# The expert loop of a decoder step: 17 turns for 18, with the used turns in the middle

## The reference

```python
def moe(h, w_router, b_router, wg, wu, wd):
    ...
    _, idx = lax.top_k(jnp.where(in_grp, sel, -jnp.inf), TOP_K)
    p_sel = jnp.take_along_axis(probs, idx, axis=-1)
    w = p_sel / jnp.sum(p_sel, axis=-1, keepdims=True)
    gates = jnp.sum(jax.nn.one_hot(idx, N_EXPERTS, dtype=jnp.float32) * w[..., None], axis=1)
    a = jnp.einsum('nd,edf->nef', t, wg)
    b = jnp.einsum('nd,edf->nef', t, wu)
    act = jax.nn.silu(a) * b * gates[:, :, None].astype(t.dtype)
    return jnp.einsum('nef,efd->nd', act, wd).reshape(shape)
```

## Time and profile before

| | |
|---|---|
| runs | 1200.85, 1202.0, 1206.45 us; median 1202.0 |
| profiled execution | span 1199.4 us from the first to the last instruction; the page gives no other time of its own for it |
| TensorE busy | 1143.6 us (95%) |
| VectorE, ScalarE, POOL busy | 618.3, 339.4, 256.3 us |
| first matmul of the loop, start of the last tile on TensorE | 804.16, 1170.61 us |
| one step of TensorE in the loop | 22.5 us |
| weight transfers in the loop, issue to landing | up 8.5, gate 9.7, down 14.0 us (medians) |
| waits of ScalarE's L1404 for TensorE | 186.4 us in 18 |
| executions of POOL's scatter L1013 | 17 |

### The profile page before, as it was taken

The page is one execution under the profiler, slowest core; times in us unless marked ns, Lnnn a source line. Parts: engine busy times, 40 slices in busy tenths (PEclk is TensorE's granted clock), DMA queues, the critical chain, the costliest instruction groups (busy, mean ns, idle before and its releaser), DMA issues.

```text
span 1199.4 us, 19161 instructions
## 1 busy us (share of the span) xinstructions
PE 1143.6 (95%) x6692; PEld 540.0 (45%) x6692; DVE 618.3 (52%) x1255; ACT 339.4 (28%) x719; POOL 256.3 (21%) x303
## 2 busy tenths in 40 slices
PE   6999999999997999998999999999999999999995
PEld 3444444444444666665544454533333333333332
DVE  0010676867779899999985574831121122122111
ACT  2132221222107888888412232100000000000000
POOL 2011102210218930000010010122223223222222
PEclk8999999999998999999999999999999999999998
DMA  9942243223328455744623356699968697968983
GB/s 358 350 151 75 98 127 116 78 97 97 98 78 277 157 195 167 239 155 162 231 87 106 105 172 224 247 343 336 352 239 315 228 359 285 352 233 295 350 292 136
DMA packets 114100, 250.76 MB, mean 209 GB/s; under 512 B 14446, under 2 KB 28910, under 8 KB 113000
## 3 DMA queue, kind: packets, MB, share of 16 engines
q1 hardware_dynamic: 93345, 206.85, 49.6%
q0 software_dynamic: 16704, 38.30, 9.1%
q10 hardware_dynamic: 3984, 4.72, 1.2%
HBM read 370.93 MB, written 38.17 MB: 341 GB/s over the span
## 4 chain that ended last, share of the span: by engine, by line
PE 68%; DVE 11%; DMA 9%; issue 6%; ACT 3%; SPq 2%; POOL 0%; POOLq 0%; DVEq 0%; ACTq 0%
PE bank L1612 21%; PE bank L2022 16%; PE bank L2036 7%; PE bank L1803 7%; DMA low<-out_dram,o_col 3%; PE bank L1592 3%; DVE big L2304 2%; DMA out_dram<-mid,o_col 2%; DVE big L2314 2%; PE bank L1467 2%; DVE cvT L2355 2%; DMA big<-in_w_up_dram 1%; PE bank L1674 1%; PE bank L2012 1%; DMA h_d<-low 1%
## 5 line engine op out<-in xcount | busy, mean ns | idle before, releaser
L2022 PE MATMUL bank<-big,mid 128*64 128x512 f32 x1104 | 251.1, 595 | 2.1 <-DMA big<-in_w_gate_dram 1.9
L1612 PE MATMUL bank<-big 128*128 128x512 f32 x560 | 249.2, 598 | 0.1
L1612 PEld LDWEIGHTS bank<-big 128*128 128x128 f32 x560 | 103.6, 190 | 131.3 <-issue 131.3
L2199 DVE SCALAR_TENSOR_TENSOR cvT<-low,cw,cvT 128x256 f32<-128x256 f32 x360 | 156.9, 512 | 0.0
L2022 PEld LDWEIGHTS bank<-big,mid 128*64 128x64 f32 x1104 | 78.1, 137 | 147.3 <-issue 147.3
L2036 PE MATMUL bank<-big,mid 128*64 128x512 f32 x544 | 119.6, 592 | 0.0
L2304 DVE TENSOR_TENSOR_SCAN big<-big 128x513 f32<-128x513 f32 (+4 forms) x96 | 91.5, 992 | 4.8 <-ACT big L1208 4.7
L2915 DVE TENSOR_TENSOR mid<-bank,low 128x512 f32<-128x512 f32 x34 | 21.9, 686 | 112.8 <-PE bank L2036 57.2
L899 POOL TENSOR_TENSOR st<-st,mhalf 128x16 f32<-128x16 f32 (+1 forms) x9 | 25.2, 2802 | 252.6 <-DVE st L2230 243.8
L2896 DVE TENSOR_TENSOR xt<-xt,bank 128x512 f32<-128x512 f32 x18 | 12.4, 688 | 126.6 <-ACT xt L1409 125.3
L2036 PEld LDWEIGHTS bank<-big,mid 128*64 128x64 f32 x544 | 39.1, 137 | 77.7 <-issue 77.7
(11 more groups left out here) (463 smaller groups left out, 1407.4 us busy)
## 6 DMA issues: line engine op xcount, KB each, us to landing
big<-in_w_gate_dram SPq DMA_DIRECT2D x38, 2048.0 KB, 9.7
big<-in_w_up_dram SPq DMA_DIRECT2D x37, 2048.0 KB, 8.5
big<-in_w_down_dram SPq DMA_DIRECT2D x37, 2048.0 KB, 14.0
low<-in_w_ada_dram SPq DMA_DIRECT2D x32, 512.0 KB, 4.1
low<-in_cache_v_dram SPq DMA_DIRECT2D x64, 256.0 KB
big<-in_w_in_dram SPq DMA_DIRECT2D x8, 1280.0 KB, 17.3
xt<-in_x_prompt_dram SPq DMA_DIRECT2D x16, 512.0 KB, 4.7
mid<-in_w_ada_dram SPq DMA_DIRECT2D x8, 1024.0 KB, 13.9
```

Of the source, the lines that this page charges most:

```text
L1612: mm = pe.matmul(bank[:, 4 if cc == 2 else cc, :], hT[:, s, k, :], w_in_sb[:, k, cc * 512:(cc + 1) * 512], start=(k == 0), stop=(k == KD - 1))
L2022: mm = pe.matmul(bank[half, 2 * s + w, :], xgT[:, s, k, half], held[x][:, k, :], start=(k == 0), stop=(k == KD - 1))
L2199: c.put(V.scalar_tensor_tensor(out, src, cw[:, ch, tap:tap + 1], out, ALU.mult, ALU.add))
```

## The change

The loop has 17 turns, and the branch in it asks whether the turn lies in a window of `pairs_used` turns, which starts at `first = (17 + 1 - pairs_used) >> 1`. `inside` tests both ends at once: each of two sums has bit 5 or higher set where its end holds. Inside the loop the number of pairs done so far comes from a register of its own, `done`, counted up at the end of a used turn, and no longer from `i`.

```diff
+        PAIRS_MAX = MP // 2 - 1
+
+        def window(pairs_used):
+
+            first = (PAIRS_MAX + 1 - pairs_used) >> 1
+            return 32 - first, first + pairs_used + 31
+
+        def inside(i, at):
+            return ((at[0] + i) & (at[1] - i)) >= 32
+
+        def counter(eng):
+
+            done = nc.alloc_registers("pairs_done", engines=[eng.engine])
+            nc.regs_mov(done, 0)
+            return done
+
+        def reached(done):
+            return nc.snap(done, min_val=0, max_val=PAIRS_MAX - 1)
+
...
-            pairs_used = pe.value_load(n_pairs[0:1, 0:1], min_val=1, max_val=MP // 2 - 1)
+            pairs_used = pe.value_load(n_pairs[0:1, 0:1], min_val=1, max_val=PAIRS_MAX)
+            at = window(pairs_used)
+            done = counter(pe)
...
             step(0, 0, 1, (wg_sb[:, 0, :, :], wg_next))
-            with pe.Fori(0, MP // 2) as i, pe.If(i < pairs_used):
-                step(2 * i + 1, 1, i + 1)
-                step(2 * i + 2, 0, i + 2)
+            with pe.Fori(0, PAIRS_MAX) as i, pe.If(inside(i, at)):
+                j = reached(done)
+                step(2 * j + 1, 1, j + 1)
+                step(2 * j + 2, 0, j + 2)
+                nc.regs_alu(done, done, 1, op=ALU.add)
```

More of the change, by code:

```diff
@@ L810, in _ @@
             sp.wait_ge(S["tiles_ready"], 3)
-            pairs_used = sp.value_load(n_pairs[0:1, 0:1], min_val=1, max_val=MP // 2 - 1)
+            pairs_used = sp.value_load(n_pairs[0:1, 0:1], min_val=1, max_val=PAIRS_MAX)
+            at = window(pairs_used)
+            done = counter(sp)
             def refill(t, now, nxt, then, gates=None):
@@ L825, in _ @@
             sp.wait_ge(S["tiles_ready"], 4)
-            with sp.Fori(0, MP // 2) as i, sp.If(i < pairs_used):
-                e = pass_experts(pass_exp, 2 * i + 1, 4)
+            with sp.Fori(0, PAIRS_MAX) as i, sp.If(inside(i, at)):
+                j = reached(done)
+                e = pass_experts(pass_exp, 2 * j + 1, 4)
                 for d in range(2):
-                    refill(2 * i + 1 + d, *e[d:d + 3])
+                    refill(2 * j + 1 + d, *e[d:d + 3])
+                nc.regs_alu(done, done, 1, op=ALU.add)
             for x in range(2):
@@ L1040, in _ @@
             pool.wait_ge(S["tiles_ready"], 3)
-            pairs_used = pool.value_load(n_pairs[0:1, 0:1], min_val=1, max_val=MP // 2 - 1)
+            pairs_used = pool.value_load(n_pairs[0:1, 0:1], min_val=1, max_val=PAIRS_MAX)
+            at = window(pairs_used)
+            done = counter(pool)
             step(0, 0, 1)
-            with pool.Fori(0, MP // 2) as i, pool.If(i < pairs_used):
-                step(2 * i + 1, 1, i + 1)
-                step(2 * i + 2, 0, i + 2)
+            with pool.Fori(0, PAIRS_MAX) as i, pool.If(inside(i, at)):
+                j = reached(done)
+                step(2 * j + 1, 1, j + 1)
+                step(2 * j + 2, 0, j + 2)
+                nc.regs_alu(done, done, 1, op=ALU.add)
             pool.wait_ge(S["y_done"], 2 * pairs_used + 4)
@@ L1415, in _ @@
             act.wait_ge(S["tiles_ready"], 3)
-            pairs_used = act.value_load(n_pairs[0:1, 0:1], min_val=1, max_val=MP // 2 - 1)
+            pairs_used = act.value_load(n_pairs[0:1, 0:1], min_val=1, max_val=PAIRS_MAX)
+            at = window(pairs_used)
+            done = counter(act)
             def turned_act(t, d):
@@ L1431, in _ @@
             step(0, 0)
-            with act.Fori(0, MP // 2) as i, act.If(i < pairs_used):
-                step(2 * i + 1, 1)
-                step(2 * i + 2, 0)
+            with act.Fori(0, PAIRS_MAX) as i, act.If(inside(i, at)):
+                j = reached(done)
+                step(2 * j + 1, 1)
+                step(2 * j + 2, 0)
+                nc.regs_alu(done, done, 1, op=ALU.add)
             last = 2 * pairs_used + 1
@@ L2888, in _ @@
             dve.sem_inc(S["tiles_ready"], 1)
-            pairs_used = dve.value_load(n_pairs[0:1, 0:1], min_val=1, max_val=MP // 2 - 1)
+            pairs_used = dve.value_load(n_pairs[0:1, 0:1], min_val=1, max_val=PAIRS_MAX)
+            at = window(pairs_used)
+            done = counter(dve)
             dve.sem_inc(S["act_done"], 1)
@@ L2928, in _ @@
             c.reset()
-            with dve.Fori(0, MP // 2) as i, dve.If(i < pairs_used):
-                step(2 * i + 1, 1, i + 1)
-                step(2 * i + 2, 0, i + 2)
+            with dve.Fori(0, PAIRS_MAX) as i, dve.If(inside(i, at)):
+                j = reached(done)
+                step(2 * j + 1, 1, j + 1)
+                step(2 * j + 2, 0, j + 2)
+                nc.regs_alu(done, done, 1, op=ALU.add)
                 c.reset()
```

## The result

| | before | changed |
|---|---|---|
| median | 1201.46 us (1200.85 to 1206.45, 4 runs) | 1216.53 us (1215.48 to 1217.19, 4 runs) |
| ratio | | 1.0102, 95% interval 1.0067 to 1.0137 |
| profiled span, mean granted clock | 1199.4 us, 0.987 | 1215.1 us, 0.980 |

The kernel is slower by 1.0%, 15.1 us between the medians, where 5.2 had been forecast. The time lies above the range of 1200.5 to 1212.5.

The account below looks back on a forecast made before the run. TensorE was taken to bound the kernel: 5.2 us ahead of the loop (3.5 hole, 1.7 slow clock), 0 behind, 0 on other engines, on the median 1202.0 us, gave 1207 us; range 1200.5 to 1212.5.

Parts of the forecast that it names:

- What bounds, how many turns, where they stand: TensorE bounds, its sequencer 4.1 us ahead of the array; eight used turns, ten skips behind become five ahead and four behind.
- What a skipped turn costs on TensorE: Register work added to each turn's head: a skipped turn costs 1.32 us (1.26 to 1.50) instead of 0.74.
- Ahead of the loop: hole of 3.5 us: Before the loop's first matmul TensorE idles 3.5 us where it idled none; with slow clock +5.2 us (3.1 to 6.3).
- Rival 1, one block of code is missing: First skip ahead jumps to unfetched code: miss of 3 us, hole 6.5 us, +9 us, 1211 us; chance 0.28.
- The slow clock: Behind the hole ahead of the loop TensorE runs at clock 0.50, adding 1.7 us (bounds 0 and 1.7).
- Behind the loop, worth 0: End hole shrinks from 3.5 to 1.4 us without slow clock; worth nothing, as VectorE waits for the gather.
- the hold of 3.02 us on POOL: Delay between POOL's issue of the last gather and its next instruction; without it the gather would land 2.5 us earlier.
- Rival 3: Lead hides most time ahead (hole 0.6 us), the gather at the end comes 2.5 us earlier: 1200 us; chance 0.20.
- Rival 2, each jump misses: Five skips ahead miss their code on both jumps, 10 x 3 us and the rest: about 1237 us; chance 0.07.
- The other engines: Skips ahead on VectorE, ScalarE, POOL and SP are hidden, SP the tightest with 1.9 us of slack: 0 us.
- The cover: SP's five turns ahead stay hidden because TensorE's release of the up weights moves 3.5 us later too.

Follow-up runs that it names:

- e1: Changed kernel with first = 0, so all nine skipped turns stand behind the used ones: 1204.46 us, ratio 0.9981 to the kernel before.
- e11: Kernel before with a loop of eight turns, so that no turn is skipped for this input: 1205.83 us, ratio 1.0010.
- e6: Changed kernel with TensorE's skipped turns all behind, the other engines' still five ahead and four behind: 1204.93 us, ratio 1.0000 to the kernel before.
- e13: The same kernel as e6, run again: 1203.73 us, ratio 1.0004 to the kernel before.
- e9: The changed kernel unaltered, run again in the same rounds as the kernel before: 1214.54 us for 1203.42, ratio 1.0093.
- e5: Changed kernel with the five skips moved from ahead of the first used turn to just after it: 1209.78 us, ratio 1.0045 to the kernel before.
- e18: Kernel before plus, ahead of TensorE's loop, a branch over 460 never-run instructions; the same as e3, run again: ratio 1.0017.
- e3: Kernel before plus, ahead of TensorE's loop, a branch over 230 transposes (460 instructions) that never run: ratio 0.9995.
- e12: Kernel before with every engine's loop counting to `pairs_used`, no condition and no skipped turn, second run of it: 1202.02 us, ratio 0.9992.
- e4: Kernel before plus, ahead of TensorE's loop, a branch over 50 transposes (100 instructions) that never run: ratio 0.9997.
- e15: Changed kernel with skips ahead on TensorE and GpSimd only, the other three engines' all behind: 1216.82 us, ratio 1.0095 to the kernel before.

## Why the prediction was wrong

- **What bounds, how many turns, where they stand.** Right: eight pairs, five skips ahead, four behind; a lead of the sequencer of 4.1 us before and 4.4 now.
- **What a skipped turn costs on TensorE.** Right: forecast 1.32 us, measured 1.42 ahead of the loop's first used turn.
- **Ahead of the loop: hole of 3.5 us.** This is the step that failed. The hole was 9.87 us. The step priced the jumps at the 214 ns of jumps over code that had run or was near, and left out that the first one now goes over a whole turn of code never fetched. That jump took 6.24 us. Without it the hole would have been about 3.8 us (814.62 - 800.31 = 14.3, less 6.24 put at 0.21, less the lead of 4.4), the forecast's 3.5.
- **Rival 1, one block of code is missing, chance 0.28.** It named the mechanism, its place and its sign in the profile. Its size was wrong: a miss was put at 3 us from the nearest short transfer (2.33 us from start to landing), which is only part of it: 3.8 us passed before the packet started. With 6.24 for the 0.21 already counted the hole is 9.5 us and the sum, with 1.7 to 2.5 for the clock, +11 to +12, 1213 to 1214, above the range's upper end of 1212.5. So even the rival, had it been the forecast, would have missed, by too low a price rather than by a wrong reason. Its chance of 0.28 rested on a count of packets, and a count can't tell how far ahead code is fetched: it is four in both kernels.
- **The slow clock.** 1.7 us forecast ahead, 1.6 measured, in other profiles up to 2.8: right in size. A hole three times as long did not cost three times the clock, since most of the slow stretch was idle.
- **Behind the loop, worth 0.** Right. The hole shrank to 1.64 us (forecast 1.4), the clock stayed at 1.00, the hold of 3.02 us on POOL came back with 3.01, and the gather sets the end. e1 and e11 say it from both sides: 8.4 us of hole or none, no measurable difference. Rival 3 falls with that. Its sum had a slip besides: the gather 2.5 us earlier is 2.24 by the rows it names (3.02 less 0.78).
- **Rival 2, each jump misses.** Fell: one long branch in eleven.
- **The other engines.** Right in the changed kernel's profile: their branches took at most 72 ns, SyncE's skips ended at 812.3 and TensorE's release came at 824.5. The cover is TensorE's own lateness, as the forecast said for SyncE. Without it (e6, e13) the up weights are late by 2.13 and 1.22 us, so the skips are not free by themselves. That they add nothing to the time is not shown: 2 to 5 us remain possible.
- **What no part foresaw:** the wait for gate weights of 3.76 us and 3.0 us of slow clock behind it, 4.4 us of the difference between the two profiles. It varies from 1.36 to 4.16 us between profiles. By e9, in the same rounds as the kernel before, the loss is 11.1 us between the medians, no more than the hole of 10.04 us and its slow clock explain; the 15.1 us of the first comparison are more than that, and between the scatter of this wait and the other engines' skips the rest is not settled.

## What to carry to other kernels

A conditional body that is skipped before it has ever run is a jump over code the sequencer has not fetched. If the body reaches beyond what has been fetched ahead (460 instructions did here, 230 did not), the first skip costs one stall of 6 to 7 us, at once and for one skip as for five; skipped after the body has run, it costs only its register work. This is measured on TensorE alone; the other engines' bodies gave no branch above 72 ns. So let the used turns of a loop come first and the unused ones behind, where a chain of transfers may hide them. Count register work against the lead of the sequencer: what goes beyond the lead leaves the array idle (e5: 6.30 us).

## What the runs showed of the hardware that I had not expected

- The stall is longer than its transfer. The packet of 16 KB took 1.0 to 1.1 us; it started 3.8 us into a branch of 6.2 (changed kernel), 3.9 of 6.35 (e9), 4.3 of 6.7 (e18). The queues moved 374 GB/s at that time, with the share of the DMA engines at 1.05; whether the wait is shorter on idle queues was not tried.
- The granted clock fell to 0.50 at 807.5, 2.8 us after the array ran dry, and rose at 817.7, 3.1 us after it had started again. Such a fall also follows waits for weights of 2.4 us and more (e3 2.41, e12 2.67, e4 2.97), but not every one (e5 2.86 and e15 2.70 had none), so a wait of this length may cost its own time or 1.3 to 3.0 us more (the matmul group behind it took 4.99 us for 3.65 in e18, 6.64 for 3.65 in the changed kernel).
